# Placing the steps beside the dense products anew in a two-block transformer kernel

## The chip, the cores and the metric

One core of a Trainium2 chip runs the whole program. The metric is the device time of one execution in microseconds (us); the kernel before took 1850.96 us, median of 3 runs. Engines are named as in the profile: PE is TensorE, DVE is VectorE, ACT is ScalarE, POOL is GpSimd, SP is SyncE.

## The reference, cut to what matters

The first block has two layers over 512 tokens of width 1024, the second block one. In a layer of the first block:

```
h = rms_norm(x, norm1);  proj = h @ w_in             # 1024 x 2764
A: latent attention   qa = rms_norm(a_cq) @ mla_w_uq;  kv = rms_norm(a_ckv) @ mla_w_ukv;  rope on 32 of 96
B: banded attention   rope(q), rope(k), window of 128 keys, a sink in the softmax
C: indexed attention  score = sum_h w[t,h] relu(q_idx[t,h] . k_idx[s]);  top 128 keys of each query
D: attention with a forget gate,  logits + cum[t] - cum[s]
x = x + concat(A, B, C, D) @ w_out
h2 = rms_norm(x, norm2)
x = x + square(relu(h2 @ w_up)) @ w_down             # 1024 x 4096, 4096 x 1024
```

The second block projects `h @ w_in_2` to three groups of queries, keys and values, attends in dilated windows of each group, mixes them by their softmax sums, and merges that with a pooled branch.

## The kernel before, in words

**Dense products.** `product` multiplies a 512-token activation by a 1024 x 512 piece of weight (a *job*). It goes through 32 *positions*: two halves of the contraction, in each four token tiles by four 128-deep slices. A position is three matmuls (L2079, L2080, L2081), because every operand is held as a high and a low part. The high part of a half weight (`w_hi`) is made by ACT in one instruction, the low part (`w_lo`) by POOL in two, as soon as `w_hi` is there; `split_high` for the next job is called `ahead`: its first half when the running job has passed position 15, its second when the running job has ended. PE executes its instructions strictly in the written order, and so do the others; semaphores tie them together.

**Hosted steps.** Small pieces of attention are written between the positions of dense jobs, so that their results travel through ACT and DVE while PE goes on with the product. On PE and on ACT a generator `side` yields after each step, and the tables `HOSTED` (first block) and `HOSTED2` (second block) say after which position of which job how many steps follow. `spread(first, end, count)` distributes a count evenly. DVE has no such table: it takes the same work in a fixed order and waits for PE and ACT.

**The steps of a layer.** First, in `JOB_A`, three turns (transposes by PE) of the index rows. Then six *index rounds* (L2187): eight recorded matmuls on PE, `Relu` on ACT, four multiply-adds into `select` on DVE (L1916, L1919); a round may start when DVE is through with the round before. After that the list `SIDE`: `L` turns the latents (queries' latents, then, as its second part in `give_more`, the keys' and values' latent `ckvT`), `U0` to `U3` multiply the latents of one token tile by the weights (L2245, L2248), `K` turns the banded queries and keys (its second part again in `give_more`), `P` are eight banded scores with their probabilities' turns and outputs, `F` sums the forget gates. `U0` waits for `ckvT`; `K` waits for DVE's rotation of all of `rows_b` (`window_ready`), which DVE does when it is through with `U3`; the first `P` waits for the second part of `K`.

In the kernel before, the second part of `L` or `K` and the start of the item after it belong to one step, so they stand back to back on PE.

**Other places.** In layer 0 PE computes a bias line with six recorded matmuls (L2316) between `JOB_IDX` and `JOB_A`; DVE copies it out of PSUM bank S (`line`, L1747), and PE waits for `line_ready` ahead of `JOB_A`. For the second norm of a layer, ACT makes `h_hi` of eight column tiles (`high_T`), then four sums of squares of X (`square_sum`, L1364), then `ahead` of the first feed-forward job. In the second block, `host_steps` places for each group of heads 2 x items + 1 steps; the first of them holds only the scores of the first item (L1059), the second begins with the turn of its probabilities (L1070), which needs DVE's bias and maxima and ACT's 16 recorded exponentials (L720).

Of the kernel before, what the change touches and what calls it, by code (L numbers as in the profile page):

```python
# [16 lines left out]
P = 128  # L17
# [3 lines left out]
TT = SEQ // P  # L21
KT = D_MODEL // P
# [24 lines left out]
HALF_K = KT // 2  # L47
# [4 lines left out]
JOB_IDX, JOB_A, JOB_B, JOB_C, JOB_D, JOB_V = range(6)  # L52
PROJ_N = (IDX_W, A_W, 512, 512, 512, 512)
PROJ_JOBS = 6
OUT_JOB = PROJ_JOBS
FFN_JOB = OUT_JOB + 2
# [9 lines left out]
TR_NORM2 = TR_IDX + 3  # L66
# [58 lines left out]
def bank_before(no):  # L125
# [20 lines left out]
SIDE = ([("L",)] + [("U", t) for t in range(TT)] + [("K",)]  # L146
        + [("P", hp, qt) for hp in range(2) for qt in range(TT)] + [("F",), ("M",)])
NS = len(SIDE)
AT = {item: n for n, item in enumerate(SIDE)}
# [3 lines left out]
def units(n):  # L153

    return {"L": ("st", "s"), "U": ("s", "s"), "K": ("st", "s"), "P": ("to", "t"), "F": ("s", ""), "M": ("s", "s")}[SIDE[n][0]]
# [23 lines left out]
def continues(n):  # L179

    return n < NS or "t" in units(n - 1)[0]


def side_steps(first, end):

    return sum(continues(n) + (n > 0 and SIDE[n - 1][0] == "P") for n in range(first, end))


def spread(first, end, count):
    return {pos: (pos - first + 1) * count // (end - first) - (pos - first) * count // (end - first)  # L190
            for pos in range(first, end)}


HOSTED = {JOB_IDX: {}, JOB_A: {18: 3, 21: 1, 25: 1, 29: 1},
          JOB_B: {1: 1, 6: 1, 11: 1, **spread(12, 32, side_steps(0, AT["K",]))},
          JOB_C: spread(14, 32, side_steps(AT["K",], AT["K",] + 3)),
          JOB_D: spread(0, 32, side_steps(AT["K",] + 3, AT["K",] + 6)),
          JOB_V: spread(0, 32, side_steps(AT["K",] + 6, AT["M",]))}

# [1 line left out]
LAYER_SC = NB + NI  # L201
LAYER_OV = NI
EARLY_ROUNDS = 9 * ROUNDS // 4
EARLY_STEPS = side_steps(1, AT["M",]) - 1


def late_rounds(i):
# [93 lines left out]


def host_steps(jobs, items, first, end):
    for pos, count in spread(first, end, 2 * items + 1).items():
        HOSTED2[jobs[pos // 32]][pos % 32] = count


# [51 lines left out]
UNITS_CREDIT, PAIR_CREDIT, IDX_CREDIT = TT, 2, 4  # L359
# [30 lines left out]
def build(nc, A, out):  # L390
    ctx = ExitStack()
    with ctx:
        def sem(name):
            return ctx.enter_context(nc.semaphore(name))
# [22 lines left out]
        gain1, gain2 = base.place("gain1", [P, KT]), base.place("gain2", [P, KT])  # L417
# [91 lines left out]
        def again(at, name, dt=F32, shape=(P, 4, SEQ)):  # L509
# [34 lines left out]
        bank_filled, bank_drained = sem("bank_filled"), sem("bank_drained")  # L544
# [22 lines left out]
        rel_ready, line_filled, line_ready, line_saved = (  # L567
            sem(n) for n in ("rel_ready", "line_filled", "line_ready", "line_saved"))
# [782 lines left out]
        def _(act):  # L1351
# [18 lines left out]
            def high_T(gain, tr, first=0, end=KT):  # L1370

                for k in range(first, end):
                    act.wait_ge(tr_filled, tr + (k + 1))
                    scale = 1.0 if gain is None else gain[:, k:k + 1]
                    act.activation(h_hi[:, k, :], S[:, k % 4, :], ACT.Copy, scale=scale).then_inc(hi_ready, 1)
# [11 lines left out]
            for l in range(DEPTH):  # L1387
                unit, tr, jobs = l * LAYER_UNITS, l * LAYER_TR, l * LAYER_JOBS
# [41 lines left out]
                def side():  # L1430

                    for n in range(3):
                        yield
                    for n in range(IDX_PRODUCTS):
                        act.wait_ge(idx_filled, l * IDX_PRODUCTS + (n + 1))
                        left = S[:, n % 4, 0:P * (n // 8 + 2)]
                        act.activation(left, left, ACT.Relu).then_inc(idx_positive, 1)
                        if n % 4 == 3:
                            yield
                    for n in range(NS + 1):  # L1440
                        if n and "t" in units(n - 1)[1]:
                            act.wait_ge(side_odd, odds + (ODD[n - 1, "t"] + 1))
                            width = P * len(window_tiles(n - 1))
                            act.activation(prob_b[(n - 1) % 2][1][:, 0:width], bank(n - 1, 1)[:, 0:width], ACT.Copy
                                           ).then_inc(odd_taken, 1)
                        if n < NS:
                            start(n)
                        if n == AT["L",]:
                            latent_roots()
                        if continues(n):  # L1450
                            yield
                        if n and SIDE[n - 1][0] == "P":
                            yield
# [151 lines left out]
                ahead(OUT_JOB + 1, 0)  # L1605
                high_T(gain2, tr + TR_NORM2, 0, HALF_K)
                ahead(OUT_JOB + 1, 1)
                high_T(gain2, tr + TR_NORM2, HALF_K, KT)
                for t in range(TT):
                    act.wait_ge(bank_drained, unit + (TT * (OUT_JOB + 1) + t + 1 + UNITS_CREDIT))  # L1610
                    ins = square_sum(t)
                ins.then_inc(sumsq_ready, 1)

# [54 lines left out]
        def _(dve):  # L1668
# [59 lines left out]
            for l in range(DEPTH):  # L1728
# [35 lines left out]
                def top_rounds(count=None):  # L1764

                    if count is None:
                        k = next(round_steps)
                        if k >= EARLY_STEPS:
                            return
                        count = (k + 1) * EARLY_ROUNDS // EARLY_STEPS - k * EARLY_ROUNDS // EARLY_STEPS  # L1770
                    for r in itertools.islice(rounds, count):
# [304 lines left out]
        def _(pe):  # L2076
# [83 lines left out]
            for l in range(DEPTH):  # L2160
                unit, tr, item0, score0 = l * LAYER_UNITS, l * LAYER_TR, l * NI, l * LAYER_SC + NB
# [11 lines left out]

                def side():

                    pe.wait_ge(idx_rows_ready, l + 1)
                    for n in range(3):
                        turn_unit(tr + (TR_IDX + n), S[:, 2 + n % 2, :],
                                  lambda t: rows_idx[:, t, P * n:P * n + P] if n < 2 else k_idx4[:, t, :])
                        yield  # L2180
                    pe.wait_ge(tr_drained, tr + (TR_IDX + 3 + PAIR_CREDIT))
                    for r in range(IDX_ROUNDS):
                        qt, first = r // 2 + 1, 4 * (r % 2)
                        pe.wait_ge(idx_drained, l * IDX_PRODUCTS + (4 * r + IDX_CREDIT))
                        for h in range(first, first + 4):
                            at = slice(32 * (h % 4), 32 * (h % 4) + 32)
                            pe.matmul(S[:, h % 4, 0:P * (qt + 1)], qiT[at, h // 4, P * qt:P * qt + P],  # L2187
                                      kiT[at, 0:P * (qt + 1)], start=True, stop=True).then_inc(idx_filled, 1)
                        yield
                    for n in range(NS + 1):  # L2190
                        if n and "t" in units(n - 1)[0]:
                            give_more(n - 1)
                        if n < NS:
                            pair_free(n)
                            start(n)
                        if continues(n):
                            yield
                        if n and SIDE[n - 1][0] == "P":
                            window_output(n - 1)
                            yield  # L2200
# [53 lines left out]
                def give_more(n):  # L2254

                    kind = SIDE[n][0]
                    if kind == "P":
                        pe.wait_ge(score_drained, l * LAYER_SC + (SCORE[n] + 1 + PAIR_CREDIT))
                        for e, filled in enumerate((side_even, side_odd)):
                            for b in range(len(window_tiles(n))):  # L2260
                                ins = pe.transpose(bank(n, e)[:, P * b:P * b + P], prob_b[n % 2][e][:, P * b:P * b + P], ident)
                            ins.then_inc(filled, 1)
                        return
                    pe.wait_ge(even_taken, evens + (EVEN[n, "s"] + 1))
                    rows, at = (rows_a, 2 * P) if kind == "L" else (rows_b, P)
                    turn_columns(bank(n, 0), lambda t: rows[:, t, at:at + P]).then_inc(side_even, 1)
# [44 lines left out]
                if l == 0:  # L2311
                    pe.wait_ge(const_loaded, 48)
                    pe.wait_ge(hot_loaded, 32)
                    pe.wait_ge(rel_ready, 1)
                    for g in range(3):
                        ins = pe.matmul(S[0:B2_H, g, 0:SKEW], rel_row[0:NUM_BUCKETS + 1, B2_H * g:B2_H * g + B2_H],  # L2316
                                        hot[0:NUM_BUCKETS + 1, g, :], start=True, stop=True)
                    ins.then_inc(line_filled, 1)
                    pe.wait_ge(line_ready, 1)
                for job in (JOB_A, JOB_B, JOB_C, JOB_D, JOB_V):  # L2320
                    project(job)

# [154 lines left out]
```

## Time and profile before

| | |
|---|---|
| runs | 1850.82, 1850.96, 1854.16 us |
| the profiled execution's own time | 1854.13 us |
| its span | 1852.3 us |
| PE busy | 1797.3 us, 97% |
| DVE, ACT, POOL busy | 919.2, 656.4, 731.4 us (50%, 35%, 39%) |
| granted PE clock, mean | 0.994 |

How to read it: PE has 55 us without a matmul in the whole span, and every other engine is idle about half of the time. An idle time written in brackets in a row is that engine's, just before the instruction, and the name behind it is what released the wait. A matmul's recorded end overlaps the start of the next, so idle time is counted from the end of the record.

### The profile page before, as it was taken

What the parts mean: (1) busy time and instruction counts of PE and PEld (TensorE: products, weight loads), DVE (VectorE), ACT (ScalarE), POOL (GpSimd) and SP (SyncE); (2) the same over time, 40 slices, a digit from 0 to 9 for tenths busy, and PEclk for the clock granted to TensorE, in tenths of its full rate; (3) what the DMA queues carried; (4) which work ended last, traced back from release to release, by engine and by line L of the source; (5) the groups of instructions that cost most, each with busy time, mean ns of one, the idle gap of its engine ahead of it and who ended that gap; (6) DMA issues with size and microseconds to landing.
All of it is one profiled execution on the core that took longest, in us unless ns stands there. A gap on an engine that the chain in (4) does not pass through costs nothing.

```text
span 1852.3 us, 22975 instructions
## 1 busy us (share of the span) xinstructions
PE 1797.3 (97%) x9055; PEld 1463.1 (79%) x9057; DVE 919.2 (50%) x1508; ACT 656.4 (35%) x1230; POOL 731.4 (39%) x328
## 2 busy tenths in 40 slices
PE   8999899999999999998999999999999999999997
PEld 7677668788888886776688888888788988888786
DVE  4679662514142346697627372727522134339374
ACT  4533552322122235345523131222435343442212
POOL 3233334444444433333444445544343434334442
PEclk9999999999999999999999999999899999999999
DMA  7225002232233233220025424243242223222211
GB/s 230 69 69 166 6 24 86 78 110 91 91 95 109 68 88 105 69 69 1 24 69 183 177 96 159 91 167 101 78 148 69 82 71 120 71 69 93 89 69 46
DMA packets 104447, 171.00 MB, mean 92 GB/s; under 512 B 21615, under 2 KB 39431, under 8 KB 103208
## 3 DMA queue, kind: packets, MB, share of 16 engines
q1 hardware_dynamic: 103320, 169.79, 27.9%
q8 instruction: 60, 0.98, 0.2%
q14 instruction: 27, 0.22, 0.0%
q10 hardware_dynamic: 1040, 0.00, 0.0%
HBM read 166.56 MB, written 7.93 MB: 94 GB/s over the span
## 4 chain that ended last, share of the span: by engine, by line
PE 83%; DVE 7%; issue 5%; POOL 2%; ACT 2%; DMA 0%; SPq 0%; DVEq 0%; POOLq 0%; ACTq 0%
PE G L2079 24%; PE G L2080 23%; PE G L2081 23%; POOL w_lo L1314 2%; PE S L2363 2%; PE S L1085 1%; PE G L2399 1%; DVE select L1919 1%; DVE neg_max L1955 1%; PE S L1059 1%; PE G L2347 1%; DVE work L1755 1%; PE S L1070 1%; PE G L2380 1%; DVE top L1754 1%
## 5 line engine op out<-in xcount | busy, mean ns | idle before, releaser
L1314 POOL TENSOR_TENSOR w_lo<-raw,w_hi 128x1024 fp32r<-128x1024 f32 (+2 forms) x268 | 661.2, 2489 | 987.7 <-ACT w_hi L1360 675.9
L2079 PE MATMUL G<-h_hi,w_hi 128*128 128x512 f32 x896 | 356.1, 397 | 4.0 <-POOL w_lo L1314 2.1
L1360 ACT ACTIVATE w_hi<-raw 128x2048 fp32r<-128x2048 f32 (+1 forms) x94 | 178.9, 1903 | 496.0 <-PE G L2081 496.0
L2081 PE MATMUL G<-h_hi,w_lo 128*128 128x512 f32 x896 | 350.0, 391 | 0.0
L2080 PE MATMUL G<-h_lo,w_hi 128*128 128x512 f32 x896 | 349.6, 390 | 0.0
L2079 PE MATMUL G<-w_hi,h_hi 128*128 128x512 f32 (+2 forms) x704 | 278.1, 395 | 3.7 <-DVE line L1747 1.4
L2081 PE MATMUL G<-w_hi,h_lo 128*128 128x512 f32 (+2 forms) x704 | 268.2, 381 | 0.0
L2080 PE MATMUL G<-w_lo,h_hi 128*128 128x512 f32 (+2 forms) x704 | 267.8, 380 | 0.0
L2079 PEld LDWEIGHTS G<-h_hi,w_hi 128*128 128x128 f32 x896 | 168.5, 188 | 42.3 <-issue 4.4
L2080 PE MATMUL G<-w_lo,u_hi 128*128 128x512 f32 x512 | 201.7, 394 | 0.0
L2079 PE MATMUL G<-w_hi,u_hi 128*128 128x512 f32 x512 | 200.7, 392 | 0.0
L2081 PE MATMUL G<-w_hi,u_lo 128*128 128x512 f32 x512 | 198.7, 388 | 0.0
L2081 PEld LDWEIGHTS G<-h_hi,w_lo 128*128 128x128 f32 x896 | 168.6, 188 | 36.0
L2080 PEld LDWEIGHTS G<-h_lo,w_hi 128*128 128x128 f32 x896 | 168.7, 188 | 34.6 <-issue 1.0
L2079 PEld LDWEIGHTS G<-w_hi,h_hi 128*128 128x128 f32 x704 | 140.7, 200 | 33.7 <-issue 11.3
L2081 PEld LDWEIGHTS G<-w_hi,h_lo 128*128 128x128 f32 x704 | 140.7, 200 | 21.3
L2080 PEld LDWEIGHTS G<-w_lo,h_hi 128*128 128x128 f32 x704 | 141.1, 200 | 20.5 <-issue 1.9
L2011 DVE SCALAR_TENSOR_TENSOR X<-G,inv_square,X 128x512 f32<-128x512 f32 x64 | 47.7, 750 | 220.0 <-PE G L2081 219.5
L2030 DVE TENSOR_TENSOR square<-relu 128x512 f32<-128x512 f32 x64 | 57.6, 900 | 154.6 <-ACT relu L1636 151.2
L698 ACT ACTIVATE w_hi<-raw 128x2048 fp32r<-128x2048 f32 x38 | 72.7, 1912 | 118.6 <-PE G L2081 118.6
L2079 PEld LDWEIGHTS G<-w_hi,u_hi 128*128 128x128 f32 x512 | 96.1, 188 | 22.5
L2081 PEld LDWEIGHTS G<-w_hi,u_lo 128*128 128x128 f32 x512 | 96.1, 188 | 21.5
(317 smaller groups left out, 2214.7 us busy)
## 6 DMA issues: line engine op xcount, KB each, us to landing
raw<-in_w_in_dram SPq DMA_DIRECT2D x40, 1024.0 KB, 5.2
raw<-in_w_up_dram SPq DMA_DIRECT2D x32, 1024.0 KB, 5.1
raw<-in_w_down_dram SPq DMA_DIRECT2D x32, 1024.0 KB, 5.1
raw<-in_w_out_dram SPq DMA_DIRECT2D x12, 1024.0 KB, 5.0
w_ada<-in_w_ada_dram SPq DMA_DIRECT2D x4, 3072.0 KB, 12.0
skew_scratch<-line_scratch SPq DMA_DIRECT2D x1, 4608.0 KB
raw<-in_w_in_dram SPq DMA_DIRECT2D x8, 512.0 KB, 4.4
raw<-in_w_in_dram SPq DMA_DIRECT2D x4, 832.0 KB, 6.8
```

The costliest lines, as they stand in the source:

```text
L698: act.activation(w_hi[:, c % SPLIT_SLOTS], raw[:, c % RAW_SLOTS], ACT.Copy).then_inc(high_ready, 1)
L1059: ins = pe.matmul(dst, queries[at, tile0 + n, q], keys[at, tile0 + n, k], start=True, stop=True)
L1070: ins = pe.transpose(S[:, 2 * (it % 2) + e, P * b:P * b + P], prob2[:, it % 2, e, P * b:P * b + P], ident)
L1085: ins = pe.matmul(dst, prob2[:, it % 2, e, P * place:P * place + P], values[:, m + 1 - blocks + b, HD * h:HD * h + HD], start=b == 0, stop ...
L1314: ins = pool.tensor_tensor(w_lo[:, c % SPLIT_SLOTS, part, 0:n], raw[:, c % RAW_SLOTS, part, 0:n], w_hi[:, c % SPLIT_SLOTS, part, 0:n].bitc ...
L1360: act.activation(w_hi[:, c % SPLIT_SLOTS, :, 0:n], raw[:, c % RAW_SLOTS, :, 0:n], ACT.Copy).then_inc(high_ready, 1)
L2011: dve.scalar_tensor_tensor(dst, G[:, t, :], factor, dst, ALU.mult, ALU.add).then_inc(bank_drained, 1)
L2030: step.done(dve.tensor_tensor(square[:], relu[:, n % 2, :], relu[:, n % 2, :], ALU.mult))
L2079: pe.matmul(dst, a_hi, b_hi, start=first, stop=False)
L2080: pe.matmul(dst, a_hi, b_lo, start=False, stop=False)
L2081: return pe.matmul(dst, a_lo, b_hi, start=False, stop=last)
L2363: pe.matmul(bank, qkT[at, p % 2, q, P * qt:P * qt + P], qkT[at, p % 2, k, P * tiles[0]:P * (qt + 1)], start=True, stop=False)
```

## The change

Five edits, none of which adds or removes an instruction that computes:

1. `HOSTED[JOB_B]` and `HOSTED[JOB_C]` get new positions. The fourth to sixth index rounds stand after positions 2, 7, 12 of `JOB_B` (before: 1, 6, 11), `L` after 17 (15), `U3` moves from the end of `JOB_B` to position 3 of `JOB_C`.
2. `parted`: behind the second part of `L` and of `K` there is one more yield on PE and ACT, so that product positions come between it and the next item.
3. `host_steps` puts the first step of each group of the second block three positions earlier.
4. ACT's four sums of squares for the second norm go one by one behind the last four `h_hi`, with one wait for all of X ahead of them.
5. PE waits for `line_ready` in the first hosted step of layer 0 (position 18 of `JOB_A`) in place of ahead of `JOB_A`.

```diff
+def parted(n):
+    return n > 0 and SIDE[n - 1][0] in ("L", "K")
...
-    return sum(continues(n) + (n > 0 and SIDE[n - 1][0] == "P") for n in range(first, end))
+    return sum(continues(n) + parted(n) + (n > 0 and SIDE[n - 1][0] == "P") for n in range(first, end))
...
-          JOB_B: {1: 1, 6: 1, 11: 1, **spread(12, 32, side_steps(0, AT["K",]))},
-          JOB_C: spread(14, 32, side_steps(AT["K",], AT["K",] + 3)),
+          JOB_B: {2: 1, 7: 1, 12: 1, 17: 1, 20: 1, 23: 1, 27: 1, 31: 1},
+          JOB_C: {3: 1, **spread(14, 32, side_steps(AT["K",], AT["K",] + 3))},
...
-EARLY_STEPS = side_steps(1, AT["M",]) - 1
+EARLY_STEPS = side_steps(1, AT["M",]) - sum(parted(n) for n in range(NS)) - 1
...
 def host_steps(jobs, items, first, end):
-    for pos, count in spread(first, end, 2 * items + 1).items():
+    places = {pos: count for pos, count in spread(first, end, 2 * items + 1).items() if count}
+    places[min(places) - 3] = places.pop(min(places))
+    for pos, count in places.items():
         HOSTED2[jobs[pos // 32]][pos % 32] = count
...
                             act.activation(prob_b[(n - 1) % 2][1][:, 0:width], bank(n - 1, 1)[:, 0:width], ACT.Copy
                                            ).then_inc(odd_taken, 1)
+                        if parted(n):
+                            yield
                         if n < NS:
                             start(n)
...
                 high_T(gain2, tr + TR_NORM2, 0, HALF_K)
                 ahead(OUT_JOB + 1, 1)
-                high_T(gain2, tr + TR_NORM2, HALF_K, KT)
+                act.wait_ge(bank_drained, unit + (TT * FFN_JOB + UNITS_CREDIT))
                 for t in range(TT):
-                    act.wait_ge(bank_drained, unit + (TT * (OUT_JOB + 1) + t + 1 + UNITS_CREDIT))
+                    high_T(gain2, tr + TR_NORM2, HALF_K + t, HALF_K + t + 1)
                     ins = square_sum(t)
                 ins.then_inc(sumsq_ready, 1)
...
                 def side():
+                    if l == 0:
+                        pe.wait_ge(line_ready, 1)
                     pe.wait_ge(idx_rows_ready, l + 1)
...
                             give_more(n - 1)
+                        if parted(n):
+                            yield
                         if n < NS:
                             pair_free(n)
                             start(n)
...
                     ins.then_inc(line_filled, 1)
-                    pe.wait_ge(line_ready, 1)
```

On PE, in `JOB_C` of layer 0, the second part of `K` (turns of `rows_b` by the identity in `masks`) and the first banded scores (from `qkT_b`) stood so before:

```order
L2081 MATMUL G<-w_hi,h_lo 128x512
L2214 MATMUL S<-masks,rows_b 128x128 x4
L2276 MATMUL S<-qkT_b 128x128 x2
L2280 MATMUL S<-window_few,ident_few 128x128 x2
L2079 MATMUL G<-w_hi,h_hi 128x512
```

and stand so now (line numbers are 10 to 14 higher; G and S are the two halves of PSUM):

```order
L2228 MATMUL S<-masks,rows_b 128x128 x4
L2089 MATMUL G<-w_hi,h_hi 128x512
L2090 MATMUL G<-w_lo,h_hi 128x512
L2091 MATMUL G<-w_hi,h_lo 128x512
L2089 MATMUL G<-w_hi,h_hi 128x512
L2090 MATMUL G<-w_lo,h_hi 128x512
L2091 MATMUL G<-w_hi,h_lo 128x512
L2089 MATMUL G<-w_hi,h_hi 128x512
L2090 MATMUL G<-w_lo,h_hi 128x512
L2091 MATMUL G<-w_hi,h_lo 128x512
L2290 MATMUL S<-qkT_b 128x128 x2
L2294 MATMUL S<-window_few,ident_few 128x128 x2
```

Three positions of the product have come between the turn and the scores. Between the second part of `L` and `U0` the same three stand now.

On ACT, from the third drain of `JOB_B`'s rows to `K` of layer 0 (`mla_k`, `mla_v` are what ACT takes of a `U`; the two `w_hi` are the halves of the next jobs), before:

```order
L1411 ACTIVATE rows_b<-G,rstd 128x512
L1474 ACTIVATE mla_k<-S,m_rstd 128x4x64
L1475 ACTIVATE mla_v<-S,m_rstd 128x256
L1411 ACTIVATE rows_b<-G,rstd 128x512
L1474 ACTIVATE mla_k<-S,m_rstd 128x4x64
L1475 ACTIVATE mla_v<-S,m_rstd 128x256
L1360 ACTIVATE w_hi<-raw 128x2048 x2
L1464 ACTIVATE qkT_b<-S 128x512
L1411 ACTIVATE rows_c<-G,rstd 128x512
```

and now:

```order
L1419 ACTIVATE rows_b<-G,rstd 128x512
L1484 ACTIVATE mla_k<-S,m_rstd 128x4x64
L1485 ACTIVATE mla_v<-S,m_rstd 128x256
L1368 ACTIVATE w_hi<-raw 128x2048
L1484 ACTIVATE mla_k<-S,m_rstd 128x4x64
L1485 ACTIVATE mla_v<-S,m_rstd 128x256
L1368 ACTIVATE w_hi<-raw 128x2048
L1474 ACTIVATE qkT_b<-S 128x512
L1419 ACTIVATE rows_c<-G,rstd 128x512 x2
```

`U3` has moved behind the `w_hi` that ends `JOB_B`, and so behind the start of POOL's two `w_lo` instructions.

On ACT at the second norm (`h_hi` from the turned X, `junk` the sums of squares, `w_hi` at the end that of the feed-forward), before:

```order
L1360 ACTIVATE w_hi<-raw 128x2048
L1375 ACTIVATE h_hi<-S,gain_57 128x512 x4
L1364 ACTIVATE junk,sumsq<-X 128x1024 x4
L1661 UNCONDITIONAL_BRANCH
L1661 ISA
L1357 ISA
L1360 ACTIVATE w_hi<-raw 128x2048
```

and now:

```order
L1368 ACTIVATE w_hi<-raw 128x2048
L1383 ACTIVATE h_hi<-S,gain_57 128x512
L1372 ACTIVATE junk,sumsq<-X 128x1024
L1383 ACTIVATE h_hi<-S,gain_57 128x512
L1372 ACTIVATE junk,sumsq<-X 128x1024
L1383 ACTIVATE h_hi<-S,gain_57 128x512
L1372 ACTIVATE junk,sumsq<-X 128x1024
L1383 ACTIVATE h_hi<-S,gain_57 128x512
L1372 ACTIVATE junk,sumsq<-X 128x1024
L1671 UNCONDITIONAL_BRANCH
```

Three of the four sums now stand ahead of the last `h_hi`; one is left between it and `w_hi`.

## Rows read from the trace of the kernel before

**Rows 1.** The page, busy time by engine: PE.

```profile
PE 1797.3 (97%) x9055; PEld 1463.1 (79%) x9057; DVE 919.2 (50%) x1508; ACT 656.4 (35%) x1230; POOL 731.4 (39%) x328
```

**Rows 2.** Waits of PE, whole span: line, releaser, us in total, times, longest.

```profile
PE S L2187 <- DVE select L1919: 3.2, 8, 0.8
...
PE S L1070 <- ACT prob L720: 2.4, 2, 1.2
PE G L2079 <- POOL w_lo L1314: 2.1, 2, 1.1
PE S L2214 <- DVE select L1919: 2.1, 2, 1.1
PE S L2276 <- DVE qkT_b L1885: 2.1, 2, 1.1
...
PE S L2245 <- issue: 1.8, 2, 0.9
...
PE G L2079 <- DVE line L1747: 1.4, 1, 1.4
```

**Rows 3.** Timeline of PE in JOB_B: start, us, instruction, idle before it.

```profile
59.78 0.93 PE L2187 MATMUL S<-kiT,qiT 32*128 32x384 f32 x8 [0.70 <-DVE select L1919]
...
74.70 1.09 PE L2214 MATMUL S<-masks,rows_a 128*128 128x128 f32 x8 [1.06 <-DVE select L1919]
...
78.14 0.39 PE L2081 MATMUL G<-w_hi,h_lo 128*128 128x512 f32 x1
78.37 0.60 PE L2214 MATMUL S<-masks,rows_a 128*128 128x128 f32 x4
79.86 1.53 PE L2245 MATMUL S<-w_uq,cqT 128*128 128x384 f32 x4 [0.89 <-issue]
```

**Rows 4.** Timeline of DVE: the copy of the second latent.

```profile
79.01 0.75 DVE L1887 TENSOR_SCALAR ckvT<-S,kv_gain 128x512 f32<-128x512 f32 x1 [2.82 <-PE S L2214]
```

**Rows 5.** Timeline of PE: U3, JOB_C's first matmul, K, first banded scores.

```profile
94.62 1.45 PE L2245 MATMUL S<-w_uq,cqT 128*128 128x384 f32 x4
...
96.37 0.80 PE L2079 MATMUL G<-w_hi,h_hi 128*128 128x512 f32 x1
...
109.72 1.04 PE L2214 MATMUL S<-masks,rows_b 128*128 128x128 f32 x8
...
115.00 0.49 PE L2276 MATMUL S<-qkT_b 64*128 64x128 f32 x4 [1.06 <-DVE qkT_b L1885]
```

**Rows 6.** Timelines of DVE and of POOL from U3 on.

```profile
96.18 0.62 DVE L1871 TENSOR_SCALAR mla_q<-S,m_rstd 128x384 f32<-128x384 f32 x1 [1.12 <-PE S L2245]
...
98.02 0.96 DVE L1718 TENSOR_TENSOR turn<-rows_b,rope 128x768 f32<-128x768 f32 x1
...
102.84 3.15 DVE L1721 TENSOR_TENSOR rows_b<-rows_b,rope 128x768 f32<-128x768 f32 x1
...
106.90 0.95 DVE L1723 TENSOR_TENSOR rows_b<-rows_b,turn 128x768 f32<-128x768 f32 x1
...
99.69 5.49 POOL L1314 TENSOR_TENSOR w_lo<-raw,w_hi 128x1024 fp32r<-128x1024 f32 x2 [19.24 <-ACT w_hi L1360]
...
109.93 4.71 POOL L1314 TENSOR_TENSOR w_lo<-raw,w_hi 128x1024 fp32r<-128x1024 f32 x2 [4.75 <-ACT w_hi L1360]
```

**Rows 7.** Timelines of ACT and of POOL at the second norm, layer 0.

```profile
326.28 0.69 ACT L1375 ACTIVATE h_hi<-S,gain 128x512 fp32r<-128x512 f32 x1 [2.51 <-PE S L2127]
326.86 1.05 ACT L1364 ACTIVATE junk<-X 128x1024 f32<-128x1024 f32 x1
...
333.00 5.17 POOL L1314 TENSOR_TENSOR w_lo<-raw,w_hi 128x1024 fp32r<-128x1024 f32 x2 [12.70 <-ACT w_hi L1360]
```

**Rows 8.** Timeline of PE: first scores of the second block's first group.

```profile
1405.32 1.16 PE L1059 MATMUL S<-qkv 64*128 64x128 f32 x16
```

**Rows 9.** Stretches: us, PE busy, granted PE clock, DMA share, GB/s.

```profile
30.00:40.00 10.00, 8.56 (x35) 0.83 0.44 136
...
1320.00:1335.00 15.00, 13.12 (x45) 0.67 0.58 157
```

## The prediction

> **What bounds the kernel now.** The page's busy times come first: PE is busy 97% of the span, every other engine half of it or less [rows 1]. So the end is set by PE, which runs one written list of instructions; time can only come out of its gaps (1852.3 - 1797.3 = 55 us in all) or out of its clock. Next I read who PE waited for [rows 2]. Seven of its rows belong to places that the change touches: 3.2 + 2.4 + 2.1 + 2.1 + 2.1 + 1.8 + 1.4 = 15.1 us of recorded idle. Other engines' idle times are of no account by themselves; they matter only where the moved steps make one of them late. Then the timelines of PE around each of these waits, to see how far ahead the released work is finished, and of DVE, ACT and POOL at the three places where a step lands somewhere new.
>
> One correction applies to each wait. A matmul's record outlives its turn in the pipeline: one that starts at 78.14 and lasts 0.39 ends at 78.53, and the next, which waits for nothing, starts at 78.37 [rows 3]. So removing a recorded wait altogether spares 0.16 us more than its record. And one position of a 512-wide job is worth (109.72 - 96.37) / 19 = 0.70 us [rows 5].
>
> **The change part by part.**
>
> *Index rounds and L.* The rounds are paced by DVE: a round may go only when DVE has finished the previous one, so PE arriving later wastes nothing. The fourth round waited 0.70 recorded, 0.86 in truth [rows 3]; the distance from the third round grows by one position, which fills 0.70 of it. The fifth and sixth keep their distance of five positions, so their share of the 3.2 us stays. L waited 1.06 + 0.16 = 1.22 for the last round [rows 3]; its distance grows from four positions to five, another 0.70, and about 0.4 us of recorded wait remains. Per layer 1.4 us, twice: **2.8 us**.
>
> *U0.* It waited 0.89, attributed to "issue"; the code says that it waits for ckvT. DVE copied that at 79.01 to 79.76 [rows 4], 1.4 us after PE began the turn at 78.37. Three positions (2.1 us) now lie between, so the wait goes: 0.89 + 0.16 = 1.05, twice: **2.1 us**. The same holds for the first banded scores behind K's second part: 1.06 + 0.16 = 1.22 [rows 5], three positions, twice: **2.4 us**. Behind them, the first probabilities' turn is now four positions (2.8 us) away instead of five; I allow 2 us for DVE's maximum and ACT's two exponentials, and ACT's queue holds only a drain ahead of them, so I cost that at nothing. If it slips, it is by tenths.
>
> *U3 moved, and K.* This is the part that can go wrong. DVE turns all of rows_b after U3, and K waits for it. Before: the rotation ended at 106.90 + 0.95 = 107.85 and K started at 109.72, 1.9 us of room [rows 5, 6]. Now U3 starts four positions into JOB_C, at 99.2 to 99.5 on the same scale (96.37 is the job's first matmul), and DVE follows 96.18 - 94.62 = 1.56 later, at 101.1, for 0.62. Then come six small turns of mla_q and the six large ones of rows_b at 0.95 each. POOL's two w_lo instructions start at 99.69 and take 4.71 undisturbed [rows 6], so until 104.4. In the old trace the two large turns that met them took about 3 us instead of 0.95 (3.15 in the row), one for each POOL instruction. Now the small turns meet them: DVE is held to about 104.5, then 0.9 for the rest of the small ones and 5.7 for the large ones: 111.1. K is one position earlier but has U3 in front of it, which costs 94.62 to 96.37 plus 0.4 of a long first matmul, 2.15: 109.72 - 0.70 + 2.15 = 111.2. It is a dead heat. Bounds: nothing lost (rotation on time), and one more POOL instruction in the way, 3.15 - 0.95 = 2.2 us per layer, or two, 4.4. POOL's next pair began at 109.93 [rows 6] and follows position 15, so it moves by the same 2.15 to 112.1, one us behind the rotation's end. I take the value nearest to the on-time end, 0.2 us per layer: **-0.4 us**.
>
> The Trainium skill ("SBUF — State Buffer", section "Who interferes with whom") says that a VectorE instruction with two SBUF inputs and a GpSimd instruction that reads SBUF exclude each other, each holding the port for its whole length. The row of 3.15 us agrees. By that rule the small turns too are held, as I assume; if only large ones were, K would have 1.5 us of room, and the sum would be 0.4 us better.
>
> *The line.* PE waited 1.4 for DVE's copy [rows 2]; with 0.16, **1.6 us**. The copy is done long before position 18 of JOB_A, and nothing between uses bank S. JOB_A's first positions need ACT's drains of JOB_IDX, which in this trace are over by the time the small matmuls end, so no wait takes its place.
>
> *Squares.* ACT's four sums of squares (1.05 each and 0.19 for the accumulator read, spaced 1.04) stood between the last h_hi and the w_hi whose w_lo PE waited for [rows 7]. ACT idled 2.51 us ahead of the last h_hi and the same ahead of the two before, so three sums fit there with 1.4 us to spare, and w_hi comes 3.1 us earlier. POOL's pair ended at 338.17, and PE had waited 1.06 for it [rows 2]; with w_lo 3 us earlier, 1.06 + 0.16 = 1.22 goes, twice: **2.4 us**. The wait for all of X costs nothing: the last part of X is written before the first of the four turned tiles arrives.
>
> *Second block.* The turn of the first probabilities waited 1.2 us in two groups [rows 2]; the scores stood seven positions earlier, at 1405.32 [rows 8]. Three positions more (2.1 us) cover it, 1.2 + 0.16 = 1.4, twice: **2.8 us**. The third group shows no such wait, and moving it gives nothing. The earlier scores need drained banks of the previous job, which ACT finishes within 1 us of its end; position 5 is 4 us in.
>
> **Sum.** 2.8 + 2.1 + 2.4 - 0.4 + 1.6 + 2.4 + 2.8 = 13.7 us. Against the profiled execution's own time, 1854.1 - 13.7 = 1840.4. That execution is the slowest of those shown; the median of the runs is 1851.0, 3.2 us below. So the median should be 1851.0 - 13.7 = **1837.3 us**. PE waits for nothing else that keeps its own time (no transfer, no fixed rate of POOL shows among its longer waits), so I expect the sum to arrive undiminished at the end.
>
> **The clock** is left out of the sum. It stood at 0.83 in 30 to 40, where the line's small matmuls (8 rows wide) and PE's wait lie, and at 0.67 in 1320 to 1335, behind small matmuls of the modulation [rows 9]; these are mixtures of the two levels, 2.4 and 1.2 GHz. Without the wait at 31 the first dip may vanish: 10 x 0.17 = 1.7 us more. One dip more elsewhere costs the same. The skill's "TensorE: Matmul & The Clock Gate", section "What's actually happening", has the level follow recent activity, which would favour the gain; I leave it in the range.
>
> **Rivals.**
> 1. *K is late.* For: the dead heat above, and one more POOL instruction in the way of the rotation costs 2.2 us. Against: POOL's next pair comes 1 us later. With one in each layer: 1837.3 + 4.4 = 1841.7; with two in each, 1846.1. It decides when the rotation runs more than 1 us later than worked out.
> 2. *The waits of the first projection come back.* If the chain through DVE (rounds, U, rotation, rounds of top-k) and not PE sets the pace of JOB_B to JOB_D, the 7.3 us of the first two groups of edits are given back at the next wait. Then 6.8 us are left: 1844.2. Against: DVE is idle 1 us and more ahead of each U (1.12 in [rows 6]).
> 3. *Slower, by the clock.* PE's small matmuls of the turns now stand in other company. The stretch from 1320 to 1335 lost 15 x 0.33 = 5 us. To end 0.2% (3.7 us) above the median of before, 13.7 + 3.7 = 17.4 us would have to be lost, 35 us at the lower level. It decides only if dips of that kind appear in both layers, at three or four new places; nothing before shows one without a run of small matmuls ahead of it.
>
> **How the numbers follow.** The forecast has 0.78, K late 0.11, waits come back 0.07, clock 0.02, 0.02 for no net effect of any other kind. 0.2% is 3.7 us, about what a measurement of this kernel can tell from no change. The forecast and the first two rivals all lie under 1847.3; with a little off for spread among runs (1850.8 to 1854.2 before), faster 0.95, same 0.03, slower 0.02. The range: the low end takes both dips of the clock of 1.7 us, 1837.3 - 3.4 = 1833.9; the high end takes rival 1 and a little of the runs' spread, 1843.
>
> **What would show it.** Among PE's waits after: L1747's, the second block's L1070's and w_lo's rows gone; the scores behind K and U0 without idle; L's wait about 0.4 us; index rounds' total down from 3.2 to about 1.8. K's turn (now L2228 on rows_b) has an idle of 0 to 0.5 us; 2 us or more there is rival 1. PE's busy time should stay at 1797 within 2 us, and its idle fall from 55 to about 42; if idle falls less while these rows are gone, the waits came back elsewhere (rival 2), and if busy rises, it is the clock.

## The result

The changed kernel takes 1860.49 us (median of 5 runs, 1858.96 to 1860.70); the kernel before, in the same session, 1851.30 (1850.82 to 1854.16). The ratio is 1.0041, 95% interval 1.0030 to 1.0051: **slower**, by 0.4% or 9.2 us between the medians. Predicted was 1837.3, range 1833.9 to 1843.0.

One sentence of the description ahead of the prediction is wrong, and the prediction took it over. The first steps of the second block do not move three positions earlier. In

```python
places[min(places) - 3] = places.pop(min(places))
```

Python evaluates the right side first. `pop` takes the first place out, and the `min(places)` on the left then finds the second. So the step goes three ahead of the *second*:

```
group of heads   before           changed          meant
first, second    8, 15, 21, ...   12, 15, 21, ...  5, 15, 21, ...
third            7, 12, 18, ...   9, 12, 18, ...   4, 12, 18, ...
```

The profile after, beginning with the page's busy times (to be held against [rows 1]) and the waits of PE ([rows 2]; lines are 8 to 14 higher, L1078 is L1070 of before, L2228 is L2214, L2199 is L2187):

```profile
span 1857.0 us, 22977 instructions
...
PE 1799.8 (97%) x9055; PEld 1464.4 (79%) x9057; DVE 921.6 (50%) x1508; ACT 657.2 (35%) x1230; POOL 729.4 (39%) x328
```

```profile
PE S L1078 <- ACT prob L728: 9.1, 3, 3.9
PE S L2228 <- DVE cqT L1871: 5.3, 2, 2.7
...
PE S L2199 <- DVE select L1929: 1.8, 6, 0.4
...
PE S L2228 <- DVE select L1929: 0.7, 2, 0.4
```

Read them in two halves. What was to go, went: there are no rows any more for w_lo, the line, the banded scores and U0, the rounds' total is 1.8 and L's own 0.7, as predicted. But L1078 did not go from 2.4 to nothing, it rose to 9.1, and a row stands there that the kernel before did not have at all: L2228 waiting for DVE's cqT. Together that is 6.7 + 5.3 = 12.0 us of new idle against 10.2 of old idle that went (rounds 1.4, L 1.4, U0 1.8, banded scores 2.1, the line 1.4, w_lo 2.1). With the small changes of other rows, PE's idle as a whole rose from 1852.3 - 1797.3 = 55.0 to 1857.0 - 1799.8 = 57.2 us.

Where the new row comes from is on DVE. Its timeline in the changed kernel, and POOL's, from the last index round on:

```profile
72.02 0.29 DVE L1933 TENSOR_TENSOR select<-select,masks 128x128 f32<-128x128 f32 x1
72.35 0.17 DVE L1795 TENSOR_SCALAR m_var<-m_sumsq 128x4 f32<-128x4 f32 x1
72.42 2.39 DVE L1796 TENSOR_SCALAR m_var<-m_sumsq 128x4 f32<-128x4 f32 x1
74.73 0.16 DVE L1800 TENSOR_TENSOR gate_z<-rows_a,gate_bias 128x16 f32<-128x16 f32 x1
74.93 2.21 DVE L1801 SCALAR_TENSOR_TENSOR gate_a<-gate_z 128x16 f32<-128x16 f32 x1
77.06 0.74 DVE L1871 TENSOR_SCALAR cqT<-S,q_gain 128x512 f32<-128x512 f32 x1
...
72.39 4.72 POOL L1322 TENSOR_TENSOR w_lo<-raw,w_hi 128x1024 fp32r<-128x1024 f32 x2 [9.16 <-ACT w_hi L1368]
```

Two operations on 4 and 16 columns take 2.39 and 2.21 us in place of 0.16: each is held for one of POOL's two instructions. cqT, which PE's second part of L needs, stands behind them in DVE's fixed order. In the kernel before the same four small operations ran at 75.01 to 75.53, and POOL began 0.2 us after their end:

```profile
75.01 0.17 DVE L1785 TENSOR_SCALAR m_var<-m_sumsq 128x4 f32<-128x4 f32 x1
...
75.36 0.17 DVE L1791 SCALAR_TENSOR_TENSOR gate_a<-gate_z 128x16 f32<-128x16 f32 x1
...
75.73 4.72 POOL L1314 TENSOR_TENSOR w_lo<-raw,w_hi 128x1024 fp32r<-128x1024 f32 x2 [9.82 <-ACT w_hi L1360]
```

The timeline of PE in the changed kernel, at L's second part and at the second block's first group:

```profile
77.86 0.66 PE L2228 MATMUL S<-masks,rows_a 128*128 128x128 f32 x4 [2.64 <-DVE cqT L1871]
...
1402.72 1.16 PE L1067 MATMUL S<-qkv 64*128 64x128 f32 x16
1410.09 1.62 PE L1078 MATMUL S<-masks,prob 128*128 128x128 f32 x8 [3.94 <-ACT prob L728]
```

From the scores to the turn of the probabilities it is 7.4 us in both kernels (before: 1405.32 [rows 8] to 1412.69): the turn waits for ACT's exponentials, and their time has not changed. With three positions between instead of seven, PE has 2.8 us less to do in it (four positions of 0.70 us), and 1.2 + 2.8 = 4.0 is about the 3.94 us that the row shows.

Behind these long waits the granted clock falls below 1.00 for a few us (called a dip here), which it did not do there before. The stretches of PE are, with columns as in [rows 9]:

```profile
75.00:80.00 5.00, 2.36 (x11) 0.93 0.31 73
80.00:85.00 5.00, 5.00 (x14) 0.73 0.39 137
...
725.00:730.00 5.00, 2.44 (x9) 0.78 0.37 105
730.00:735.00 5.00, 5.00 (x17) 0.88 0.30 106
...
1410.00:1415.00 5.00, 4.91 (x29) 0.66 0.00 0
...
1495.00:1500.00 5.00, 1.94 (x18) 0.92 0.02 5
1500.00:1505.00 5.00, 5.00 (x24) 0.73 0.00 0
```

Each such dip is worth 1.7 us of PE's time: 5 x (0.07 + 0.27) at 75 to 85, 5 x (0.22 + 0.12) at 725 to 735, 5 x 0.34 at 1410, 5 x (0.08 + 0.27) at 1495 to 1505. There is one behind each of the four long waits (L's two, of 2.64 and 2.67 us, and those of 3.94 and 3.93 us at L1078), 6.8 us together. In the kernel before the same places stand at 1.00. Elsewhere the profiled execution of the changed kernel lost less than that of before: the dip at 30 to 40 and one at 180 to 190 (1.7 us each) are gone, that of 1315 to 1335 fell from 5.1 to 1.7 us, and one of 1.7 us came at 830. So PE's busy time rose by 2.5 us only. Why the dips away from the long waits come and go is not shown.

### The profile page after: what moved, and what is told of

Same layout as the page of the kernel before. It is cut to its first block, busy times and chain, and to the rows that moved or that the text cites. A ratio compares the mean times of both kernels' runs of the same rounds, so it can differ in the third digit from the quotient of the medians.

```text
span 1857.0 us, 22977 instructions
## 1 busy us (share of the span) xinstructions
PE 1799.8 (97%) x9055; PEld 1464.4 (79%) x9057; DVE 921.6 (50%) x1508; ACT 657.2 (35%) x1230; POOL 729.4 (39%) x328
## 4 chain that ended last, share of the span: by engine, by line
PE 89%; DVE 7%; ACT 2%; issue 1%; DMA 0%; SPq 0%; DVEq 0%; ACTq 0%
PE G L2089 26%; PE G L2090 25%; PE G L2091 25%; PE S L2376 2%; PE S L1093 1%; PE G L2412 1%; DVE select L1929 1%; PE S L1067 1%; DVE neg_max L1965 1%; PE S L2137 1%; PE G L2360 1%; PE S L1078 1%; DVE work L1765 1%; PE G L2393 1%; DVE top L1764 1%
```

## The experiments

Two causes are proposed. **A1**: the misplaced first steps of the second block. **A2**: POOL's w_lo holds DVE's small operations ahead of cqT. The rival **R** is that the clock falls by itself in the new order, and for A2 **R2**, that L's turns or ACT's half of them are what is late. The kernel before gave 1852.53 us in the session of e1 to e4, 1852.44 in that of e5 to e7 and 1853.17 in that of e8 and e9.

**e1_host_undone**: the change, without the edit of host_steps.

```diff
-    places = {pos: count for pos, count in spread(first, end, 2 * items + 1).items() if count}
-    places[min(places) - 3] = places.pop(min(places))
-    for pos, count in places.items():
+    for pos, count in spread(first, end, 2 * items + 1).items():
```

> The changed kernel with the first steps of the second block back at their old positions (8, 8 and 7 of their jobs). In the changed kernel they stand at 12, 12 and 9, later than before and not three earlier, because the right side of the assignment empties the first place before the left side asks for the smallest key. Theory A (that misplacement and a wait for DVE behind L, in both layers, make the loss): PE's waits at L1078 fall from 9.1 to about 2.4 us, plus one or two dips of the clock of 1.7 us less behind them: 1860.5 - 6.7 - 1.7 to 3.4 = 1850 to 1852. Rival R (PE's clock falls at new places by itself, whatever the waits): the waits go but the dips stay, about 1854. The two waits of 2.7 us behind L stay under both.

Measured 1848.20 us (1846.81 to 1851.47), ratio to before 0.9979 (0.9970 to 0.9988). Without that single edit the loss is a small gain: 12.3 us below the changed kernel, or 9.2 + 4.3 = 13.5 us when each is held against the kernel before of its own session. Its waits of PE:

```profile
PE S L2226 <- DVE cqT L1869: 5.3, 2, 2.7
...
PE S L1076 <- ACT prob L726: 2.4, 2, 1.2
```

The waits account for 6.7 us, and the two dips behind them, which are gone too, for 3.4. Of the 13.5 us some 3 are left that the profiles do not show; e2 comes back to them. A1 holds, and R falls, which had the dips stay and the time at 1854. The wait behind L is untouched, with its dips at 75 to 85 and 725 to 735, as both said.

**e2_host_alone**: the kernel before, with only that edit as the change has it.

```diff
-    for pos, count in spread(first, end, 2 * items + 1).items():
+    places = {pos: count for pos, count in spread(first, end, 2 * items + 1).items() if count}
+    places[min(places) - 3] = places.pop(min(places))
+    for pos, count in places.items():
```

> The kernel before with only the edit of host_steps, as it is in the change. Theory A: two waits grow from 1.2 to about 3.9 us and a third of 1.3 us appears, 6.7 us, plus one or two clock dips of 1.7 us behind the long waits: 1851.3 + 6.7 + 1.7 to 3.4 = 1860 to 1862, so this edit alone makes the changed kernel slower than before. Rival R: below 1859.

Measured 1866.07 us (1863.03 to 1866.80), ratio 1.0072 (1.0058 to 1.0086): 13.5 us slower than before, more than the 8 to 10 that I had worked out. Its profile (of the execution at 1863.03) has the same 9.1 us in the waits of PE (L1072):

```profile
PE S L1072 <- ACT prob L722: 9.1, 3, 3.9
```

Stretches of its PE, columns as above, around the second of these waits (3.93 us, until 1501.69):

```profile
1495.00:1500.00 5.00, 2.76 (x19) 0.97 0.46 167
1500.00:1505.00 5.00, 3.31 (x20) 0.50 0.02 5
1505.00:1510.00 5.00, 5.00 (x26) 0.85 0.13 23
```

Here the clock loses 5 x (0.03 + 0.50 + 0.15) = 3.4 us of PE's time; about 1 us of it falls into the wait itself (PE starts at 1501.69) and costs nothing.

A1 is confirmed in direction and place, and R, which asked for less than 1859, falls. The price of 13.5 is not all in the profile: the waits grew by 6.7, and the dips behind them cost some 4 (1.7 at 1410 to 1420, and about 2.4 here), which leaves about 3 us. The profiled execution is the fastest of the five, with a mean granted clock of 0.992; the three at 1866.07 to 1866.80 had 0.989. So the missing 3 us go with a lower clock in the other executions.

**e3_host_early**: the kernel before, with the first steps really three earlier.

```diff
-    for pos, count in spread(first, end, 2 * items + 1).items():
+    places = {pos: count for pos, count in spread(first, end, 2 * items + 1).items() if count}
+    at = min(places)
+    places[at - 3] = places.pop(at)
+    for pos, count in places.items():
```

> The kernel before with the first steps really three positions earlier (5, 5 and 4). My prediction's term: two waits of 1.2 us recorded, 1.4 us in truth, vanish: 1851.3 - 2.8 = 1848.5. Rival (the chain through DVE and ACT is limited by something else there, so that a wait reappears at the next turn): 1851.

Measured 1849.80 us (1848.11 to 1851.66), ratio 0.9988 (0.9979 to 0.9997): 2.7 us less, against 2.8 predicted. The row of L1070 (L1073 here) is gone from the waits. So that term of the prediction was right for the edit as it was meant.

**e4_cq_first**: e1, and DVE takes cqT ahead of the latents' small operations.

```diff
-                latent_norms()
                 for n in range(AT["M",]):
...
                     if n < NS:
                         start(n)
+                    if n == AT["L",]:
+                        latent_norms()
```

> As e1_host_undone, and DVE takes the turned latent (cqT) out of PSUM ahead of its four small operations of latent_norms, not behind them. Theory A2 (in the changed kernel POOL's w_lo, 3 us earlier than before against L, holds these small operations for 4.5 us, and cqT stands behind them): PE's waits of 2.7 us behind L vanish, at most 0.7 us of them comes back at U0, which now waits for the second latent; with a dip of the clock less in each layer 1.7 us each: e1 - 4 to e1 - 8 us, about 1844. Rival R2 (L's own turns or ACT's half of them are what PE waits for): no change against e1.

Measured 1841.19 us (1839.07 to 1844.31), ratio 0.9945 (0.9932 to 0.9959), 7.0 us less than e1. DVE's timeline:

```profile
72.28 0.75 DVE L1869 TENSOR_SCALAR cqT<-S,q_gain 128x512 f32<-128x512 f32 x1 [0.50 <-PE S L2227]
72.95 1.37 DVE L1793 TENSOR_SCALAR m_var<-m_sumsq 128x4 f32<-128x4 f32 x1
74.24 0.16 DVE L1794 TENSOR_SCALAR m_var<-m_sumsq 128x4 f32<-128x4 f32 x1
74.31 2.37 DVE L1798 TENSOR_TENSOR gate_z<-rows_a,gate_bias 128x16 f32<-128x16 f32 x1
```

and POOL's:

```profile
71.89 4.75 POOL L1320 TENSOR_TENSOR w_lo<-raw,w_hi 128x1024 fp32r<-128x1024 f32 x2 [9.18 <-ACT w_hi L1366]
```

cqT (from PSUM) runs undisturbed beside POOL; two of the small ones are still held (1.37 and 2.37 us), but PE no longer waits for what stands behind them: the row of 5.3 us is gone, and U0 waits 0.9 us in all. This shows that what PE waits for is the order on DVE, and R2's "L's own turns" falls.

**e5_cq_first_host_early**: e4 with e3's places.

> All five edits of the change, with the first steps of the second block really three positions earlier, and with DVE's order at L as in e4_cq_first. If the effects add, e4_cq_first's 1841.2 less the 2.7 us that e3_host_early gave against before: 1838.5, which is near the 1837.3 that was predicted for the change. Rival (the gain of one is given back by the other): 1841.

Measured 1841.38 us (1838.21 to 1841.66), ratio 0.9932 (0.9919 to 0.9946). By the time, which is the rival's 1841, it looks as if e3's gain were lost. The page says otherwise: PE's idle is 1839.6 - 1796.1 = 43.5 us, against 1838.7 - 1792.5 = 46.2 in e4. The waits did add, 2.7 us; the clock took it back, in this execution by 3.6 us of PE busy time. The three executions at 1841.38 to 1841.66 had a mean granted clock of 0.993, the two at 1838.21, near the expected 1838.5, 0.995 and 0.996. The page's row of busy times:

```profile
PE 1796.1 (98%) x9055; PEld 1462.9 (80%) x9057; DVE 924.2 (50%) x1508; ACT 657.0 (36%) x1230; POOL 730.0 (40%) x328
```

**e6_squares_line**: the kernel before with edits 4 and 5 alone (the diff is that of the change).

> The kernel before with only the sums of squares between the turns and PE's wait for the line moved into the first hosted step. My prediction's terms: two waits for w_lo, 2.4 us, and the wait for the line, 1.6 us: 4.0 us less than before, and the clock's dip at 30 to 36 us may go, 1.7 us more: 1852.5 - 4.0 to 5.7 = 1847 to 1848.5. Rival (PE is held at the next job by the relus, which stand behind the same w_hi on ACT): 1850.

Measured 1844.92 us (1843.89 to 1846.90), ratio 0.9959 (0.9946 to 0.9973): 7.5 us less. PE's idle fell by 4.0, from 55.0 to 1843.0 - 1792.0 = 51.0, as large as the two terms together; the rest is busy time, 1797.3 to 1792.0 (the page's row):

```profile
PE 1792.0 (97%) x9055; PEld 1459.6 (79%) x9057; DVE 919.5 (50%) x1508; ACT 657.1 (36%) x1230; POOL 730.9 (40%) x328
```

No dip of the clock stands at 30 or at 180 in it. The first was foreseen as a possible gain; nothing in these two edits says why the second went. Held against e1, this experiment also says that edits 1 and 2 as made cost time: e1, which has them besides, takes 3.3 us more.

**e7_pool_later**: e1, with POOL kept away from L; DVE's order is the change's.

```diff
-                        if pos == 15 and job != JOB_IDX:
+                        if pos == 15 and job not in (JOB_IDX, JOB_B):
                             ahead(job, 0)
...
                             next(steps)
+                        if pos == 17 and job == JOB_B:
+                            ahead(job, 0)
```

> As e1_host_undone, but ACT makes the first half of w_hi for the job after JOB_B behind the step of L, not after position 15, so that POOL's two w_lo instructions start some 6 us later. DVE's order is that of the change. Theory A2 (POOL's instructions hold DVE's small operations): the latter take 0.2 us each again and PE's waits behind L are gone, about e1_host_undone - 5 to - 8 us, 1840 to 1843, unless POOL meets U0's turns and holds them. Rival R2 (DVE's order or ACT's half of L is the cause, whatever POOL does): the waits of 2.7 us stay, 1848.

Measured 1839.38 us (1837.87 to 1840.98), ratio 0.9926 (0.9912 to 0.9939), 8.8 less than e1, and 0.6 us below what A2 expected. The timelines of DVE and of POOL:

```profile
71.70 0.16 DVE L1796 TENSOR_SCALAR m_var<-m_sumsq 128x4 f32<-128x4 f32 x1
71.78 0.17 DVE L1800 TENSOR_TENSOR gate_z<-rows_a,gate_bias 128x16 f32<-128x16 f32 x1
71.98 0.18 DVE L1801 SCALAR_TENSOR_TENSOR gate_a<-gate_z 128x16 f32<-128x16 f32 x1
72.07 0.75 DVE L1871 TENSOR_SCALAR cqT<-S,q_gain 128x512 f32<-128x512 f32 x1
...
78.21 2.38 DVE L1826 SCALAR_TENSOR_TENSOR log_f<-gate_z,gate_a 128x16 f32<-128x16 f32 x1
...
78.17 4.72 POOL L1320 TENSOR_TENSOR w_lo<-raw,w_hi 128x1024 fp32r<-128x1024 f32 x2 [15.65 <-ACT w_hi L1366]
```

With POOL at 78.17 the same operations in the same order take 0.16 to 0.18 us. The hold has moved to log_f, where nothing of PE's stands behind. A2 holds and R2 falls: DVE's order was the change's, and neither the wait nor the dips at 75 and 725 are there.

**e9_rounds_back**: e1 with the index rounds back at 1, 6, 11 and L still at 17.

```diff
-          JOB_B: {2: 1, 7: 1, 12: 1, 17: 1, 20: 1, 23: 1, 27: 1, 31: 1},
+          JOB_B: {1: 1, 6: 1, 11: 1, 17: 1, 20: 1, 23: 1, 27: 1, 31: 1},
```

> e1_host_undone with the index rounds of JOB_B back after positions 1, 6, 11, all else as there: L still after 17. Theory A2: position 15 is now four positions behind the last round and not three, so POOL's w_lo starts 0.7 us later against DVE, at the edge but behind the small operations (in the changed kernel POOL began at 72.39, they would need until 72.9). The waits of 2.7 us behind L go, and the fourth round's wait of 0.7 us comes back in each layer: e1's 1848.2 - 5.3 + 1.4 = 1844.3, down to 1841 with the clock's dips. Rival R2: 1849.6, the waits behind L stay and the fourth round's come back.

Measured 1839.97 us (1838.97 to 1841.55), ratio 0.9934 (0.9920 to 0.9947), 8.2 less than e1. The timelines of DVE and of POOL:

```profile
73.51 0.17 DVE L1799 SCALAR_TENSOR_TENSOR gate_a<-gate_z 128x16 f32<-128x16 f32 x1
...
73.89 4.76 POOL L1320 TENSOR_TENSOR w_lo<-raw,w_hi 128x1024 fp32r<-128x1024 f32 x2 [9.83 <-ACT w_hi L1366]
```

POOL now begins 0.2 us behind the last small operation. So one position, the very "index rounds one later" that was to spare 0.7 us per layer, is what let POOL in. The rounds' total is back at 3.2 us, and L no longer waits at all. A2 expected 1844.3, or 1841 with fewer dips; it came out 1 us below that, and R2's 1849.6 falls.

**e8_pool_later_host_early**: e7 with e3's places; everything as meant, POOL out of the way.

> e7_pool_later with the first steps of the second block really three positions earlier: all five edits as they were meant, with POOL's w_lo out of the way of L. The waits add: e7's 1839.4 less 2.7 = 1836.7, if the clock's dips stay as they are; up to 1840 if one or two more dips of 1.7 us come, as in the profile of e5_cq_first_host_early.

Measured **1835.74 us** (1833.15 to 1838.01), ratio 0.9910 (0.9896 to 0.9924): the fastest version, 17.4 us below before. PE's idle is 1833.5 - 1791.2 = 42.3 us, and the scores and the turn of the first group stand without a wait in PE's timeline:

```profile
1387.30 1.16 PE L1068 MATMUL S<-qkv 64*128 64x128 f32 x16
...
1395.33 1.03 PE L1079 MATMUL S<-masks,prob 128*128 128x128 f32 x8
```

## Why the prediction was wrong

- **Second block, -2.8 us: the step that failed first.** "The scores stood seven positions earlier ... Three positions more (2.1 us) cover it". The term was worked out for a place that the change does not produce. In its place the waits grew by 6.7 us (L1070 2.4 to L1078 9.1), a difference of 9.5 us in this term alone, and e2 puts the edit's whole price at 13.5. I worked out the new place from the source as I read it, and did not count the positions in the order of the built program, where they are seven before and three now. For the meant edit the term was right, 2.7 measured (e3).
- **Rounds and L, -2.8 us, and U0, -2.1: right terms, a missed follower.** The rounds' rows fell by 1.4 and L's by 1.4, U0's row is gone. But "PE arriving later wastes nothing" looked at PE and DVE only. ACT's w_hi follows position 15 of the job, POOL's w_lo follows that, and position 15 had come 0.7 us nearer to the last round. The prediction followed POOL for K, at the job's end, and not here. The room had been 0.2 us. Cost: 5.3 us of wait, twice 2.7, plus two dips of the clock, 3.4 us; e4, e7 and e9 each remove it in another way, for 7.0 to 8.8 us.
- **K behind U3, -0.4: right, by a narrow margin.** K stands without an idle in both layers, and no row of a wait for rows_b exists. The timelines of DVE and of PE in the changed kernel, at the rotation, which ended at 107.11 + 0.95 = 108.06, and at K:

```profile
99.23 2.44 DVE L1729 TENSOR_TENSOR turn<-mla_q,rope 128x64 f32<-128x64 f32 x1
...
107.11 0.95 DVE L1733 TENSOR_TENSOR rows_b<-rows_b,turn 128x768 f32<-128x768 f32 x1
...
108.41 1.03 PE L2228 MATMUL S<-masks,rows_b 128*128 128x128 f32 x8
```

  One small turn was held (2.44 us in place of 0.22, after one of 0.39) and the large ones ran free at 0.95 each, so rival 1 did not come. The room was 0.35 us: the dead heat of the prediction, which fell on the good side.
- **Banded scores -2.4, squares -2.4, line -1.6: right.** Their rows are gone; e6 gives 4.0 us of idle for the last two together, the sum of the terms.
- **The clock.** It was kept out of the sum and used for a gain of up to 3.4 us at the low end. It works on both sides: the waits of 2.64, 2.67, 3.93 and 3.94 us in the changed kernel were each followed by a dip of 1.7 us, while the two waits of 1.22 us that stood at two of these places before had none behind them. The experiments switch the dips with the waits: e1 has only L's two of each, e2 only the second block's two, e8 none at these places. In e6 and e8 the gain went beyond the waits (7.5 for 4.0; 17.4 for 12.7). Rival 3 was right that the kernel gets slower and that dips come at new places, and its chance of 0.02 was too small. But it had the whole loss come from the clock, behind small matmuls; here the waits come first, 12.0 us of them, and the four new dips, 6.8 us, stand behind the longest.
- **The sum as a whole.** It gave about 42 us of idle for the meant change, and e8, which has POOL moved besides, has 42.3, so no wait came back elsewhere (rival 2). Its gain in time is 17.4 us against the 13.7 of the sum; the idle gives 12.7 of it, the rest is the clock. That e8's 1835.7 lies so near the predicted 1837.3 is partly luck, since the kernel before took 1853.17 in that session and not 1851.0.

What the profiles leave over: between the medians the changed kernel lost 9.2 us, between the profiles 4.7 (idle 2.2, busy 2.5), because the profiled execution of before is as slow as the slowest of its five and that of after is the fastest of its. The runs of one kernel differ by their clock. The 21 runs of the kernel before beside e1 to e4 lie near 1850.9, 1852.6 and 1854.1, in steps of about one dip's 1.7 us, at mean granted clocks of about 0.995, 0.994 and 0.993; those of the changed kernel go from 1858.96 at 0.992 to 1860.7 at 0.990. So the rest of the loss, like the 3 us of e2, goes with dips in the executions that were not profiled. Where these dips stand, and so whether they follow the long waits, is not shown.

## What to carry to other kernels

When steps are moved by a table, count their distance in the order of the built program, on the engine that waits, before pricing anything; reading the code that fills the table is not enough. A step moved along one engine moves against everything that the same job triggers on the others: list those followers (here ACT's w_hi and POOL's w_lo behind position 15) and look for an operation of DVE that now falls beside POOL, however small, with something urgent queued behind it. Take what the next engine waits for out first, and do the small sums after (here what was taken first came from PSUM and was not held itself).

## What the runs showed of the hardware

- Operations of DVE on 4 to 16 columns, from SBUF to SBUF, took 2.2 to 2.4 us in place of 0.16 when they met a POOL instruction of 2.36 us, one hold for each; a copy of 512 columns from PSUM beside the same POOL instruction kept its 0.75 us. One of the held ones is a TENSOR_SCALAR with a single SBUF tensor (L1796, 2.39 us), not only those with two. The Trainium skill ("SBUF — State Buffer", section "Who interferes with whom") names both kinds as blocked by a GpSimd instruction: two SBUF inputs, and a tensor_scalar where it runs in a mode that uses both ports. The trace agrees that both are held; which mode L1796 ran in, it does not say.
- The clock has a price in both directions: a mean granted clock of 0.66 over 5 us at 1410, between stretches at 1.00, right behind a PE wait of 3.94 us. The same work in e8, without the wait, ran at 1.00. In the changed kernel each wait of 2.64 to 3.94 us cost its own time and 1.7 us more. In e2 one of 3.93 us was followed by 3.4 us, of which about 1 fell into the wait.
